# Four modulation units of a hybrid decoder trunk, from the even output projection into the even attention

## The reference

```python
def ada_modulate(c, w, b):
    m = jax.nn.silu(c) @ w + b
    shift, scale, gate = jnp.split(m, 3, axis=-1)
    return shift[:, None], scale[:, None], gate[:, None]

def reference(...):
    for i in range(DEPTH):
        j = i // 2
        shift, scale, gate = ada_modulate(c, ada_w[i, 0], ada_b[i, 0])
        h = rms_norm(x, norm_g[i, 0]) * (1.0 + scale) + shift
        if i % 2 == 0:
            mix = even_mixer(h, rel_bias, ev_w_in[j], ev_w_out[j], ...)
...
```

## Time and profile before

| | |
|---|---|
| median of three timed runs | 2040.44 us (2040.06 to 2041.08) |
| the profiled execution | 2041.9 us |
| its span, first to last instruction | 2040.2 us |
| mean granted clock of TensorE | 0.982 |
| PE busy | 1927.7 us, 94% |
| PEld busy | 1658.4 us, 81% |
| DVE busy | 1541.6 us, 76% |
| ACT busy | 1062.8 us, 52% |
| POOL busy | 226.5 us, 11% |

### The profile page before, as it was taken

The page is one execution under the profiler, slowest core; times in us unless marked ns, Lnnn a source line. Parts: engine busy times, 40 slices in busy tenths (PEclk is TensorE's granted clock), DMA queues, the critical chain, the costliest instruction groups (busy, mean ns, idle before and its releaser), DMA issues.

```text
span 2040.2 us, 34283 instructions
## 1 busy us (share of the span) xinstructions
PE 1927.7 (94%) x11632; PEld 1658.4 (81%) x11632; DVE 1541.6 (76%) x2426; ACT 1062.8 (52%) x2265; POOL 226.5 (11%) x318
## 2 busy tenths in 40 slices
PE   6799988899999999999999899999999999999998
PEld 5378745666899999987777778787799999997787
DVE  6788816778678888888888788788777777778554
ACT  2255546655555555555445456575655555556443
POOL 2210002550100000000011000162000000000000
PEclk9999997999999999999999999989999999999999
DMA  9989993667688888867997877878577767665555
GB/s 375 384 317 322 324 309 119 229 217 258 214 272 278 266 287 265 285 225 269 336 334 248 288 259 213 282 253 319 167 241 240 228 212 224 212 205 167 176 189 176
DMA packets 211132, 519.53 MB, mean 255 GB/s; under 512 B 25185, under 2 KB 43058, under 8 KB 186162
## 3 DMA queue, kind: packets, MB, share of 16 engines
q1 hardware_dynamic: 182962, 316.25, 48.5%
q0 software_dynamic: 28032, 201.44, 27.1%
HBM read 515.50 MB, written 2.10 MB: 254 GB/s over the span
## 4 chain that ended last, share of the span: by engine, by line
PE 74%; DVE 13%; DMA 9%; ACT 3%; issue 2%; POOL 0%; DVEq 0%; SPq 0%; ACTq 0%; POOLq 0%
PE ps L1056 12%; PE ps L1052 12%; PE ps L1053 11%; PE ps L948 10%; PE ps L944 10%; PE ps L945 10%; DVE acc L1721 6%; DVE ring_lo L1807 3%; DMA ring<-in_od_w_in 1%; DMA first_ring<-in_ada_w 1%; DMA ring<-in_ev_w_in 1%; PE ps L760 1%; DMA ring<-in_ffn_w_down 1%; PE ps L1148 1%; DMA aring<-in_ada_w 1%
## 5 line engine op out<-in xcount | busy, mean ns | idle before, releaser
L1260 ACT ACTIVATE ring_hi<-ring 128x512 fp32r<-128x512 f32 (+2 forms) x1152 | 690.6, 621 | 593.2 <-DMA ring<-in_ffn_w_up 236.1
L1807 DVE TENSOR_TENSOR ring_lo<-ring,ring_hi 128x512 fp32r<-128x512 f32 (+2 forms) x1152 | 742.3, 681 | 287.5 <-ACT ring_hi L1260 286.0
L1052 PE MATMUL ps<-hT_hi,ring_hi 128*128 128x256 f32 x2048 | 514.1, 284 | 6.1 <-issue 5.0
L1053 PE MATMUL ps<-hT_lo,ring_hi 128*128 128x256 f32 x2048 | 508.7, 280 | 0.0
L1052 PEld LDWEIGHTS ps<-hT_hi,ring_hi 128*128 128x128 f32 x2048 | 386.2, 189 | 7.3 <-issue 6.2
L1053 PEld LDWEIGHTS ps<-hT_lo,ring_hi 128*128 128x128 f32 x2048 | 388.7, 190 | 0.0
L1056 PE MATMUL ps<-hT_hi,ring_lo 128*128 128x256 f32 x2048 | 330.1, 282 | 2.5 <-DVE ring_lo L1807 2.5
L1721 DVE SCALAR_TENSOR_TENSOR acc<-aring,cs,acc 128x2048 f32<-128x2048 f32 x126 | 296.4, 2352 | 38.2 <-DMA acc<-in_ada_b 16.7
L1056 PEld LDWEIGHTS ps<-hT_hi,ring_lo 128*128 128x128 f32 x2048 | 280.0, 188 | 3.0 <-DVE ring_lo L1807 3.0
L644 POOL DMA_DIRECT2D aring<-in_ada_w x176 | 94.9, 539 | 1365.8 <-DVE acc L1721 1339.7
L945 PE MATMUL ps<-ring_hi,hT_lo 128*128 128x512 f32 (+2 forms) x640 | 243.9, 382 | 0.0
(11 more groups left out here) (247 smaller groups left out, 2071.5 us busy)
## 6 DMA issues: line engine op xcount, KB each, us to landing
aring<-in_ada_w POOLq DMA_DIRECT2D x176, 1024.0 KB, 7.0
ring<-in_ffn_w_up SPq DMA_DIRECT2D x512, 256.0 KB, 3.1
ring<-in_ffn_w_down SPq DMA_DIRECT2D x256, 256.0 KB, 3.1
ring<-in_od_w_in SPq DMA_DIRECT2D x112, 256.0 KB, 4.1
ring<-in_ev_w_in SPq DMA_DIRECT2D x80, 256.0 KB, 5.3
first_ring<-in_ada_w POOLq DMA_DIRECT2D x16, 1024.0 KB, 7.4
ring<-in_ev_w_out SPq DMA_DIRECT2D x64, 256.0 KB, 3.4
ring<-in_od_w_out SPq DMA_DIRECT2D x64, 256.0 KB, 3.5
```

The costliest lines, as they stand in the source:

```text
L1052: nc.tensor.matmul(o[q], hi, hT_hi[:, kt, :], start=start, stop=False, skip_group_check=True)
L1053: nc.tensor.matmul(o[q], hi, hT_lo[:, kt, :], start=False, stop=False, skip_group_check=True)
L1260: ins = nc.scalar.activation(out_, in_, f, **kw)
L1807: put(v.tensor_tensor(ring_lo[:, g, part], ring[:, g, part], ring_hi[:, g, part].bitcast(F32), ALU.subtract), lo_ok)
```

## The change

One line of the table that says which attention steps carry a modulation unit, read by VectorE's `attention` and by GpSimd's loop of loads:

```diff
         def unit_in_step(n_sub, m):
 
-            return m % 2 == 1 or m in (8, 16, 24) if n_sub == 0 else m % 4 != 3
+            return m % 2 == 1 or m % 4 == 0 and m > 0 if n_sub == 0 else m % 4 != 3
```

## The result

The changed kernel takes **2049.51 us** (median of 14 runs, 2043.74 to 2056.4). The kernel before, in runs beside it on the same chip, takes 2042.62 (14 runs, the three known ones among them). The ratio is 1.0037, 95% interval 1.0025 to 1.0050: 7.6 us longer (5.1 to 10.2). The forecast of 2046.1 had the sign and a difference (5.7) inside that interval, but its range ended at 2048.8, under the measured time.

What follows compares the result with a forecast made beforehand. VectorE was taken to be what the attention waits for in a good part of its time. Stalls 2.0 + 1.4 + 2.5 - 1.4 = +4.5 us, plus 1.2 for the clock, gave 2040.44 + 5.7 = 2046.1 us; range 2042.4 to 2048.8.

Steps and rivals of the forecast that it cites:

- Steps 12, 20 and 28: Attention stretches that gain a unit: 0.42, 0.42 and 0.60 us longer, together +1.4 us.
- Step 4: Attention: the added unit makes step 5's unit wait for its load, and what follows comes 2.0 us later.
- Projection: Output projection: one of four removed units had a TensorE wait of 1.41 us behind it, so -1.4 us.
- The tail: Steps 32 to 37: late loads delay the last head's remainder and TensorE's last two products, +2.5 us.
- I take 6.9: Tail: landing time in us assumed for step 35's load, from the same load in the earlier trace.
- +3.6: Tail: upper bound in us, for the longest load landing seen, 8.0 us.
- The clock: TensorE's clock falls in quiet places lengthened around step 5 and in the tail: +1.2 us.
- I take one added fall: TensorE's clock: one more fall to the lower level, at +1.2 us, bounds 0 and 3.2.
- The forecast's other sum: Whole change: 4.5 us of stalls plus 1.6 us for each fall of TensorE's clock.
- Two falls and a slower landing: Rival, two clock falls or one in full and a slower load landing: +7.7 us, 2048.1 us; chance 0.14.
- The rival on the other side: Attention's stops take all added units, only the projection's 1.4 us gain is left: 2039.0 us; chance 0.06.

Runs made afterwards that it cites:

- e6: The change with its last modulation unit at step 37 instead of 35; 2048.76 us, ratio 1.0016 to the kernel before.
- e5: The change plus small 128x128 products on TensorE in its quiet places in the attention; 2041.76 us, ratio 0.9992 to the kernel before.
- e4: The kernel before with the projection's second unit moved from weight tile 10 to 7, all four units kept there; 2040.85 us, ratio 0.9985.
- e2: The kernel before with step 37's unit moved to step 32, the projection keeping its four; 2046.46 us, ratio 1.0020.
- e1: The change without a unit at step 32, step 37 keeping its unit, none in the projection; 2049.46 us, ratio 1.0021 to the kernel before.
- e8: The change run again, unaltered; 2051.03 us, ratio 1.0035 to the kernel before.
- e10: The change plus 23 eight-column products (46 TensorE instructions) near 81 us; 2042.27 us, ratio 0.9996 to the kernel before.
- e11: The kernel before with the projection's second unit moved from weight tile 10 to 7, plus 46 TensorE instructions near 81 us; 2034.17 us, ratio 0.9958.
- e3: The kernel before with step 37's unit moved to step 4; 2044.56 us, ratio 1.0005.
- e9: The kernel before plus 23 eight-column products (46 TensorE instructions) near 81 us; 2034.93 us, ratio 0.9970.
- e12: The kernel before plus 8 eight-column products (16 TensorE instructions) near 81 us; 2045.49 us, ratio 1.0023.
- e7: The kernel before with the projection's second unit at weight tile 7, plus small products before steps 0 to 3 and 35; 2035.81 us, ratio 0.9964.

## Why the prediction was right in sign and short in size

**Steps 12, 20 and 28 (+1.4): right.** 16.49 became 16.92 (+0.43), and so from step 19 to 23 (16.48 to 16.92, +0.44). Where the clock held (e6), steps 27 to 31 took 16.92, +0.61. Together 1.48. (Not every stretch with a unit took 16.91 before: steps 23 to 27 took 17.10, and take 16.94 now.)

**Step 4 (+2.0): right.** The wait for the load was 0.59, and with the clock held (e5) the stretch grew by 2.03.

**Projection (-1.4): right**, for the reason given: -1.61 in the change, -1.63 in e4, where no unit leaves the projection.

**The tail (+2.5): mechanism right, too small.** The step that failed is "I take 6.9": step 35's load took 7.9 us to land and step 33's 5.9 instead of 5.1. Both were issued when forecast: 464.60 and 469.14 are the 455.28 and 459.81 of the earlier trace rows, moved by the 9.32 us by which step 31 comes later. So the last head's products began 3.3 us late, close to the +3.6 that I had written for a landing of 8.0. Where the loads landed in 5.1 and 6.8 us (e2) they began 2.2 late, so the working was right for its landing. Why the loads landed later is open. (466.99, from which I counted, is the loading of the weights; the product itself began at 467.21.)

**The clock (+1.2): the step that failed** is "I take one added fall". The profile of the change has three more than before. Their prices: 0.90 in steps 3 to 7 (15.28 - 14.38), 1.41 in steps 27 to 31 (18.33 - 16.92), and 1.68 on the attention's last products (4.45 - 2.77). That is 4.0 instead of 1.2. I had named two places, the ones where waits were added; the third, at 456 us, lies in steps 27 to 31, which I had priced without one. Of the six profiles with the units of the change up to step 31 the clock fell well inside this stretch in four (the change, e1, e5 and e8), and not in e6, though the order of the work up to there is the same. In e10 the stretch is as long (18.50) for another reason: its mean clock is 0.98, and step 29's unit waits 1.44 us for its load (the unit is line 1723 in that kernel):

```profile
453.97 2.35 DVE L1723 SCALAR_TENSOR_TENSOR acc<-aring,cs,acc 128x2048 f32<-128x2048 f32 x1 [1.44 <-DMA aring<-in_ada_w]
```

Nor does such a fall need the change's units: e2 and e11 have one in steps 23 to 27, and e3 one at 457 us, where the order of the work is that of before. What decides it stays open.

**The sum.** 2.0 + 1.5 + 3.3 - 1.6 + 4.0 = 9.2 us. The profiles of the change give +9.1 from step 0 to the end of the projection (207.61 against 198.53), e8 +8.3, e10 against e9 +9.2; the ratio gives 7.6 (5.1 to 10.2). The forecast's other sum, 4.5 + 1.6 for each fall, gives 9.3 with the three falls that the trace shows. That is near by luck: the stalls were 5.2, and the falls cost 0.9, 1.4 and 1.7. The Trainium skill (TensorE: Matmul & The Clock Gate, "What's actually happening") says that the lower level is the default, which activity releases. The trace agrees for the last fall, ahead of which TensorE was busy 0.15 us of 2. Two falls and a slower landing, given 0.14, came nearest.

**The base.** Of the 3.4 us between 2046.1 and 2049.51, the base is 2.2: three runs of before gave 2040.44, and beside the change it took 2042.62. Single runs of before lie between 2030.88 and 2054.16 in what was run later, on two chips. The stages here agree to some tenths of a us between profiles where the clock does the same; what scatters is outside them: from the projection's end to the end of the span, the eight profiles with the two stops differ by up to 7.5 us (1512.2 in e8, 1519.7 in e6). A range of 6.4 us around a base of three runs was too narrow for that alone.

**The rival on the other side** (the units fit into the stops) fell where it was said to fall: the loads did not land before VectorE asked.

## What to carry to other kernels

Price a moved instruction by a stretch of the same kernel that has it already: the three stretches priced in that way came out within 0.1 us in all. Then ask of each added wait what is queued behind it and at what clock TensorE goes on afterwards; here the second was the larger part of what was missing (2.8 us of 3.5), and one unit moved two steps later (e6), behind the last work that anybody waits for, took away both in the tail.

When a kernel with extra or fewer instructions runs at another time, look where the time went before believing the reason for which they were put in: here 7.7 us came from loading code again in a loop 1100 us further on, and the list of DMA queues shows it. A control that adds the same number of instructions in an idle place tells it apart.

## What the runs showed that I had not expected

- 46 more TensorE instructions ahead of a loop run by a register remove two stops of 2.2 and 2.4 us and 18 packets of code, and 16 more turn two stops into four. Behind both stops of before the granted clock also falls (0.96 over the 40 us around the first, 0.91 in e12 with two, 1.00 in e9), but not behind every stop: in the change it is 1.00 from 1640 to 1700 us, around a stop of 2.30. Which number of instructions is best was not tried.
- Keeping the clock up does not always pay: in steps 0 to 3 the small products of e7 held it at 1.00 for some 5 us where before had 0.50, and these steps took 12.75 us instead of 11.90.
- Taking step 35's unit out of the way of the last head (e6) made the tail 1.15 us shorter than before, with 15.36 us of VectorE's work against 16.33 and no fall of the clock.
